# Cross-attention: the product of weights and values from high and low parts, one beat later, seven beats per query slab

## The reference

```python
q = (h @ w_q).reshape(B, T, 4, 256)
k, v = jnp.split(mem_n @ w_kv, 2, axis=-1)
s = jnp.einsum('bthd,bmhd->bhtm', q, k) * (256 ** -0.5)
p = jax.nn.softmax(s, axis=-1)
o = jnp.einsum('bhtm,bmhd->bthd', p, v).reshape(B, T, 1024)
return o @ w_o
```

## Time and profile before

| | |
|---|---|
| time, median of 3 runs | 1691.23 us (1691.15 to 1692.78) |
| span of the profiled execution | 1689.5 us |
| PE busy | 1673.6 us, 99% of the span |
| DVE busy | 1047.3 us, 62% |
| ACT busy | 739.1 us, 44% |
| PE's part of the chain that ended last | 88% |

### The profile page before, as it was taken

The page is one execution under the profiler, slowest core; times in us unless marked ns, Lnnn a source line. Parts: engine busy times, 40 slices in busy tenths (PEclk is TensorE's granted clock), DMA queues, the critical chain, the costliest instruction groups (busy, mean ns, idle before and its releaser), DMA issues.

```text
span 1689.5 us, 23254 instructions
## 1 busy us (share of the span) xinstructions
PE 1673.6 (99%) x9421; PEld 1404.4 (83%) x9421; DVE 1047.3 (62%) x1565; ACT 739.1 (44%) x1137; POOL 187.3 (11%) x163
## 2 busy tenths in 40 slices
PE   9999999999999999999999999999999999999998
PEld 7787887987898888888888888888898888888887
DVE  7889787474389449549675642655574545454445
ACT  6654467653553323213543323323364645253463
POOL 0455461200200000000100000000100000000001
PEclk9999999999999999999999999999999999999999
DMA  6111134421223223322322313313222222222221
GB/s 216 62 43 63 51 101 135 137 78 50 75 67 121 100 75 113 101 86 100 119 88 80 96 56 106 100 57 112 69 72 76 75 76 87 75 87 76 85 77 50
DMA packets 45576, 147.67 MB, mean 87 GB/s; under 512 B 5024, under 2 KB 8992, under 8 KB 45472
## 3 DMA queue, kind: packets, MB, share of 16 engines
q1 hardware_dynamic: 45472, 146.21, 26.5%
HBM read 144.09 MB, written 2.10 MB: 87 GB/s over the span
## 4 chain that ended last, share of the span: by engine, by line
PE 88%; DVE 8%; ACT 2%; issue 1%; DMA 0%; POOL 0%; SPq 0%; DVEq 0%; ACTq 0%
PE ps L502 22%; PE ps L504 22%; PE ps L503 22%; PE ps L507 21%; DVE sl L2052 1%; DVE ps L2112 1%; DVE y L2467 1%; DVE xl L2484 1%; DVE h L2477 0%; PE ps L1128 0%; ACT sh L1307 0%; DVE ps L2262 0%; DVE ps L2106 0%; DVE pad L2104 0%; DMA raw<-in_wqkv 0%
## 5 line engine op out<-in xcount | busy, mean ns | idle before, releaser
L1307 ACT ACTIVATE sh<-raw 128x1024 fp32r<-128x1024 f32 x257 | 268.3, 1053 | 373.1 <-PE ps L504 254.4
L2052 DVE TENSOR_TENSOR sl<-raw,sh 128x1024 fp32r<-128x1024 f32 x257 | 321.6, 1258 | 131.5 <-ACT sh L1307 131.4
L502 PE MATMUL ps<-xh,sh 128*128 128x512 f32 (+1 forms) x664 | 263.1, 396 | 0.0
L504 PE MATMUL ps<-xl,sh 128*128 128x512 f32 (+1 forms) x664 | 254.0, 382 | 0.0
L503 PE MATMUL ps<-xh,sl 128*128 128x512 f32 (+1 forms) x664 | 253.7, 382 | 0.0
L502 PE MATMUL ps<-sh,xh 128*128 128x512 f32 x384 | 151.8, 395 | 0.0
L503 PE MATMUL ps<-sh,xl 128*128 128x512 f32 x384 | 149.6, 390 | 0.0
L504 PE MATMUL ps<-sl,xh 128*128 128x512 f32 x384 | 149.6, 390 | 0.0
L502 PEld LDWEIGHTS ps<-xh,sh 128*128 128x128 f32 x664 | 124.9, 188 | 26.2 <-issue 2.4
L504 PEld LDWEIGHTS ps<-xl,sh 128*128 128x128 f32 x664 | 124.8, 188 | 24.9
L503 PEld LDWEIGHTS ps<-xh,sl 128*128 128x128 f32 x664 | 125.0, 188 | 22.7 <-issue 0.7
(11 more groups left out here) (429 smaller groups left out, 3317.5 us busy)
## 6 DMA issues: line engine op xcount, KB each, us to landing
raw<-in_wup SPq DMA_DIRECT2D x44, 512.0 KB, 3.5
raw<-in_wdn SPq DMA_DIRECT2D x24, 512.0 KB, 3.5
raw<-in_rqk SPq DMA_DIRECT2D x16, 512.0 KB, 3.9
raw<-in_rv SPq DMA_DIRECT2D x16, 512.0 KB, 3.4
raw<-in_rg SPq DMA_DIRECT2D x16, 512.0 KB, 4.4
raw<-in_rout SPq DMA_DIRECT2D x16, 512.0 KB, 3.5
raw<-in_sv SPq DMA_DIRECT2D x16, 512.0 KB, 3.4
raw<-in_sg SPq DMA_DIRECT2D x16, 512.0 KB, 3.5
```

The costliest lines, as they stand in the source:

```text
L502: e.matmul(dst, wh, ah, start=start, stop=False, skip_group_check=True)
L504: return e.matmul(dst, wh, al, start=False, stop=stop, skip_group_check=True)
L1307: e.activation(SH[j % NSPL][:], RAW[j % NRAW][:], ACT.Copy).then_inc(*hi(j))
L2052: e.tensor_tensor(SL[j % NSPL][:], RAW[j % NRAW][:], SH[j % NSPL][:].bitcast(F32), ALU.subtract).then_inc(*lo(j))
```

## The change

The values are kept in two parts. ACT now writes the high part (VMH, on the same memory, type fp32r), and DVE computes the low part VML from the bank in PSUM and VMH (`mem_v_lo`, four instructions). The banks 0 to 3 are released by DVE (`vml`) in place of ACT (`vma`). The transposed weights are kept in two parts in the same way: ACT writes PTH, DVE subtracts it from the bank and writes PTL, two instructions a head, and banks 4 and 5 are released by DVE. The product becomes `three`, so a head has 12 single-pass matmuls in place of 4 plain ones. There is one `yield` more between transposes and product in all three programs, and a query slab has seven beats in place of six.

```diff
-        VM = QK0[:].rearrange("p a t -> p (a t)").rearrange("p (b c) -> p b c", b=2)
+        VMH = VH[:].rearrange("p a t -> p (a t)").rearrange("p (b c) -> p b c", b=2)
...
+            VML = under("vml", [128, 2, 1024], F32R)
...
-            PT = alloc(ph, "pt", [128, 2, T])
+            PTH = alloc(ph, "pth", [128, 2, T], F32R)
             SX = alloc(ph, "sx", [128, 16])
+            PTL = alloc(ph, "ptl", [128, 2, T], F32R)
...
             tokens(32, MX, "m", (0, 1), nb=2)
-            rel[0], rel[1] = [(vma, (0, 0))], [(vma, (0, 1))]
+            rel[0], rel[1] = [(vml, (0, 0))], [(vml, (0, 1))]
             tokens(36, MX, "m", (2, 3), nb=2)
-            rel[2], rel[3] = [(vma, (1, 0))], [(vma, (1, 1))]
+            rel[2], rel[3] = [(vml, (1, 0))], [(vml, (1, 1))]
...
                     t.then_inc(*axm(("t", h, mb)))
-                    rel[B] = [(axa, ("pt", h, mb))]
+                    rel[B] = [(axv, ("pl", h, mb))]
+                yield
                 yield
                 for et in range(2):
                     B = 4 + et
                     b = bank(B)
                     for mb in range(2):
-                        pe.wait_ge(*axa[("pt", h, mb)])
-                        pe.wait_ge(*vma[(h // 2, mb)])
+                        pe.wait_ge(*axv[("pl", h, mb)])
+                        pe.wait_ge(*vml[(h // 2, mb)])
                         c = slice(h * 256 + et * 128, h * 256 + et * 128 + 128)
-                        t = one(b[:], VM[:, mb, c], PT[:, mb, :], mb == 0, mb == 1)
+                        t = three(b[:], VMH[:, mb, c], VML[:, mb, c], PTH[:, mb, :], PTL[:, mb, :], mb == 0, mb == 1)
...
-                slab(48 + m, X, "b1", beats=6, at_bank=[QB[m]])
+                slab(48 + m, X, "b1", beats=7, at_bank=[QB[m]])
...
-                    e.activation(PT[:, mb, :], PS[4 + mb][:], ACT.Copy).then_inc(*axa(("pt", h, mb)))
+                    e.activation(PTH[:, mb, :], PS[4 + mb][:], ACT.Copy).then_inc(*axa(("pt", h, mb)))
+                yield
                 yield
...
+            def mem_v_lo(cg):
+                for tb in range(2):
+                    c = slice(cg * 512, cg * 512 + 512)
+                    ve.wait_ge(*vma[(cg, tb)])
+                    ve.wait_ge(*onv[(1, "sq", 1)])
+                    e.scalar_tensor_tensor(VML[:, tb, c], PS[2 * cg + tb][:], LNC[:, 2 + tb:3 + tb],
+                                           VMH[:, tb, c].bitcast(F32), ALU.mult, ALU.subtract).then_inc(*vml((cg, tb)))
...
+            mem_v_lo(0)
             for g in range(4):
...
+            mem_v_lo(1)
             for lane in (bg, fg, side):
                 lane.drain()
...
-                for _ in range(4):
-                    yield
+                for _ in range(3):
+                    yield
+                for mb in range(2):
+                    ve.wait_ge(*axa[("pt", h, mb)])
+                    if h:
+                        ve.wait_ge(*axm[("o", h - 1, 1)])
+                    e.tensor_tensor(PTL[:, mb, :], PS[4 + mb][:], PTH[:, mb, :].bitcast(F32), ALU.subtract).then_inc(
+                        *axv(("pl", h, mb)))
+                yield
+                yield
```

More of the change, by code:

```diff
@@ L384, in program @@
         kmv, vma, gtv, gta = sig("mem_k"), sig("mem_v"), sig("gate_vec"), sig("gate_act")
+        vml = sig("mem_v_lo")
         lnv, lna, lnp, lnq = sig("ln_vec"), sig("ln_act"), sig("ln_ps"), sig("ln_sq")
@@ L393, in program @@
                    x2h, x2l, sq, sa, cs, ms, pw, dg, rw, rb, hs, zero, hvp, yr, out_ps, hva, cv, cva, wabh, wabl, lgt, lgp, dcv, dca, vtp, vts,
-                   gmm, gdv, gac, ggp, memh, meml, memq, mems, glv, gla, tpd, tpa, tpp, kmv, vma, gtv, gta, lnv, lna, lnp,
+                   gmm, gdv, gac, ggp, memh, meml, memq, mems, glv, gla, tpd, tpa, tpp, kmv, vma, vml, gtv, gta, lnv, lna, lnp,
                    lnq, onv, onp, onq, ya, yv, hv, axm, axv, axa, ffv, ffa, rtv, rta, rtm, rtg, stv, sta, stm]
@@ L1606, in mem_v @@
                     ac.wait_ge(*pw["mem"])
-                    e.activation(VM[:, tb, cg * 512:cg * 512 + 512], PS[2 * cg + tb][:],
+                    e.activation(VMH[:, tb, cg * 512:cg * 512 + 512], PS[2 * cg + tb][:],
                                  ACT.Copy, scale=LNC[:, 2 + tb:3 + tb]).then_inc(*vma((cg, tb)))
@@ L1742, in scalar_program @@
             for m in range(4, 8):
-                beat(6)
+                beat(7)
                 ahead(53 + m)
```

## The result

| | before | after |
|---|---|---|
| time, median (lowest to highest) | 1691.94 us (1691.15 to 1694.30), 6 runs | 1697.55 us (1696.35 to 1701.31), 6 runs |
| ratio, with its 95% interval | | 1.0034 [1.0024, 1.0044] |
| profiled execution: span | 1689.5 us | 1695.7 us (its time is 1697.5) |

The changed kernel is slower by 5.6 us on the same chip. The forecast was 4.3 us, and 1697.55 lies 0.35 us above the upper end of its range. The forecast stood on 1691.23 us for the kernel before, the median of three runs; with six runs it is 1691.94, so 0.7 us of the distance between 1697.55 and the forecast's 1695.5 is not the change.

The account below looks back on a forecast made before the run. PE was taken as the bound, busy for 99% of the span. -1.4 (attention) + 4.2 (bank 2) + 1.5 (clock) = +4.3 us: 1691.2 + 4.3 = 1695.5, own range 1694.6 to 1696.4, whole range 1690.8 to 1697.2.

Parts of the forecast that it names:

- PE's work: Attention products: twelve matmuls at 0.228 us take 2.74 in place of 3.43, saving 0.69 us a head, 2.8 in four.
- The attention: All four heads, PE's saving less new waits: 0.3 + 0.7 + 0.7 - 0.3 = 1.4 us gained.
- rival 3: Heads 1 and 2: the 0.2 us margins break and products wait for a low part; +2 more, 1697.5; chance 0.10.
- The values: Values of the memory: DVE's added instructions release bank 2 late, PE waits some 3.5 us; shift 4.2 us.
- filling: PE after any wait: 0.14 us to fill again, on top of the wait's length.
- Rival 2: Bank 2: no wait there, only the attention's gain; 1689.8 to 1690.5 us; chance 0.12.
- The clock: In or just behind the bank 2 wait: PE's clock falls to 1.2 GHz, costing 1.5 us, between 0 and 1.6.

Follow-up runs that it names:

- e6_best2: Changed kernel with slab 42 in bank 6, first two vml behind the sums of squares, head 3's transposes and product earlier on PE; 1690.63 us, ratio 0.9991.
- e1_bank6: Changed kernel with one edit: slab 42 goes into bank 6 in place of bank 2; 1692.61 us, ratio 0.9999.
- e4_off_path: Changed kernel with slabs 40 to 42 in banks 6, 7 and 5 and all four vml behind the work PE waits for; 1692.16 us, ratio 0.9994.
- e8_last_head: Changed kernel with the last two vml behind the four scalings, ahead of the last head's low part; 1696.37 us, ratio 1.0022.

## Why the prediction was wrong where it was

**PE's work: right.** A product lasts 2.78 us against the forecast 2.74, so a head gives 0.65, not 0.69. The 216 ns that the forecast quotes (the Trainium skill, TensorE: Matmul & The Clock Gate, section Back-to-back issue gap) are the page's figure for an isolated matmul; for a sustained row of weight loads and matmuls of 512 columns it gives about 131 ns. The rows here have 228 and agree with neither. The sum did not use it.

**The attention: right, 1.2 instead of 1.4.** Head 0 waited 0.17 us for `pm` (forecast 0.2), heads 1 and 2 had no wait, so rival 3 did not come. Head 3 waited 0.98 us for `ptl`, and that wait could be moved away, as e6_best2 shows.

**The values: right, 4.5 instead of 4.2.** The sum of squares was 0.67 us late (forecast 0.5), slab 42's copy came at 291.80 (291.6), the wait for `vml` was 3.3 (3.5). The whole shift by the late release is 0.93 + 3.31 + 0.26 = 4.50. About two of the three tenths are the pace of `vml`, 0.66, where I took the 0.60 of the nearest row from PSUM and named 0.66 as the other end (by the formula that I used for 0.60, that row gives 0.68). The rest is filling: 0.14, read from one row, covers only what comes behind the first start. Rival 2 is out: e1_bank6 shows what no wait would have given, and PE was 3.3 us from it.

**The clock: right in kind, too small.** This is the step that failed: "Part of it may fall into the wait; I take 1.5, between 0 and 1.6." It cost 1.6 us in the shorter case and 2.8 in the longer, so my upper end was the shorter case. The error was to take the one spell of low clock that the trace had, at the start, for the largest possible one. That row shows what one spell cost in one execution, not how long a spell can last. The starts of the later profiles would have warned: the same 16 records at the start take from 5.11 us (after) to 6.75 (e4_off_path), that is 1.5 to 3.1 above 3.62, where I had one value, 1.6. The clock column is no help there: it has 1.00 from 0 to 10 us of before, so only the records speak for a low clock at the start. Behind the wait the low pace lasted 8 or 14 matmuls, from execution to execution. With 1.6 the sum is -1.2 + 4.5 + 1.6 = +4.9, with 2.8 it is +6.1; the medians of the two measurements, 5.6 and 5.6 us above those of before, lie between.

**What was luck.** 1697.55 is 6.3 us above the 1691.23 that the forecast started from, and 5.6 above the six runs of before. With the first median the same loss would have ended at 1696.8, inside the range. The size of the clock term was wrong either way: with an upper end of 2.8 for it in place of 1.6 the forecast's own range, 1694.6 to 1696.4, would have ended at 1697.6.

What stays open: why the spell is of one or the other length in a given execution (no run set it), how often each length comes (the changed kernel has three profiles), and what a wait between 1.34 and 2.69 us, the nearest two that ran, would do here.

## What to carry to other kernels

Cheaper matmuls are worth their price only if the vector work that makes their operands does not stand between a bank and its next user: look up who is the next to write the bank, and what the releasing engine has in its queue ahead of the release. Price a new wait of a matrix engine that is busy all the time as wait plus clock: here nothing on top of 1.3 us (one profile), and 1.6 to 2.8 us on top of 2.7 to 3.4, a price that changes from execution to execution. Giving the next user another bank cost three lines and gave back 6.40 of the 7.33 us; moving the release up the queue gave back 5.33 and handed a part of the delay to the next consumer.

## What was not expected of the hardware

The clock fell with PE shown busy, in a stage that the change does not touch. In the stage of the delta rule, with many short matmuls, single profiles have a granted clock of 0.87 over 10 us in which PE is busy for 10.00 of 10, and before has 1.00 there at 9.80 of 10; the same work took some 1.4 us more (the mean's matmul at 278.79 in e6_best2 and at 277.40 before), and up to 4.8 us more in e4_off_path, where the clock was 0.83, 0.77 and 0.88 in three such windows. No run here shows what starts such a spell.

A fall need not lie at the wait: in e8_last_head four or five matmuls ran at full pace behind the wait before the pace halved.
